# The output projection of a hybrid diffusion layer: the first 128 tokens' products ahead of the others, on four PSUM banks, one weight block read twice

## The chip, the cores and the metric

The kernel runs on one core of one Trainium2 chip. The metric is the device time of one execution in microseconds (us), from the first to the last instruction of the core. All numbers are fp32.

## The reference, cut to what matters

One layer over 256 latent tokens (two blocks of 128, t = 0 and 1, in the kernel) of width 2048. A mixing sub-layer (Fourier groups and a bidirectional state-space mixer, with 256 context tokens ahead of it) is projected by `w_out` and added; then an expert layer: each token picks 16 of 16384 experts in each of 8 heads, by top-16 over two sets of 128 keys, and needs the rows `u` and `v` of each expert picked.

```python
y_x = concatenate([fourier_branch(proj_x), y_x_ssm], -1) @ w_out      # (256, 2048) @ (2048, 2048)
x = x + gm_x * rms_norm(y_x, g_post_mix)
hx2 = modulate(rms_norm(x, g_pre_ffn), sf_x, cf_x)
# peer_ffn, for each block tb of 128 tokens:
q = (tb @ w_query).reshape(128, 8, 128)
s1, s2 = q[..., :64] . sub_keys_1, q[..., 64:] . sub_keys_2
idx, gate = top 16 of the sums of the top 16 of s1 and of s2, softmax
act = gelu(einsum('td,thkd->thk', tb, expert_u[idx]))
y_f = einsum('thk,thkd->td', gate * act, expert_v[idx])
x = x + gf_x * rms_norm(y_f, g_post_ffn)
```

The mean in `rms_norm(y_x)` runs over all 2048 columns of a token, so nothing behind the projection can start for a block of tokens before all four of its column blocks are there.

## The kernel before, in words

The program is written engine by engine, each engine's instructions in the order in which it executes them, with semaphores between them. Nothing is reordered: where an engine waits, all that is queued behind it waits too.

*The projection.* `w_out` is used in four column blocks n = 0..3 of 512 (4 MB each). A product (n, t) is 16 matmuls 128x128 by 128x512 into one PSUM bank, 8 over the Fourier half and 8 over the state-space half of the mixed channels. `OUT_ORDER` (L116) gives the order: (0,0), (0,1), (1,0), (2,0), (3,0), (1,1), and, behind the start of the query stage for t = 0, (2,1), (3,1). Product (n, t) goes to bank (n % 2) * 2 + t. ScalarE reads each finished product twice (`wo_out`, L858: squares with their sum at L862, copy at L863), but not before the last tile of `w_mod` has been used (`tail_used`, VectorE, L1155), since the two share memory. Two of the products have column sums of those `w_mod` tiles in their middle (`SUMS_AT`), which the vector of the second normalisation needs.

*The weights.* Wide blocks come through two ring slots of 4 MB (`RING`, L92; slot 0 or 1 by the index's parity), each in 4 loads of 1 MB issued by SyncE (`ring_load`, L370), as soon as the last product that used the slot's former block is done. Block 2 of `w_out` has places of its own (`apart`). The ring holds `w_out` blocks 0, 1, 3 (slots 1, 0, 1) and then the two halves of `w_query`: the first (heads 0 to 3) in slot 0, the second (heads 4 to 7) in slot 1. The first head's columns alone have a load of their own (`first_head`), for a query that comes early. SyncE's queue goes on with two stores of x1 behind the query blocks. A row of such a block is 512 numbers, 2 KB.

*Behind the projection.* `x1_make(t)` (VectorE, L1357) needs all four products of t; then ScalarE squares x1 (`x1_norm`, L871), VectorE makes h2 (`x1_variance`, `h2_make`), TensorE transposes h2 (L1960) and makes queries (L1977) and key scores (L1985). For t = 0 only head 0's query is made first, TensorE then does (2,1) and (3,1), and then the queries in the order `QUERIES`: heads 1, 2, 3 of t = 0, the transposes of h2 for t = 1, heads 0 to 3 of t = 1, heads 4 to 7 of both. ScalarE has `x1_norm(1)` in its program behind the evacuation of the second query (`query_out(1)`, L903).

*The stream.* VectorE routes unit 0 (head 0, t = 0; top-16 and indices), and from then on GpSimd gathers expert rows by indirect DMA (L594): one gather is 128 rows of 8 KB, 1 MB. Each u row is used by one dot product on VectorE (`dot`, L1449). The first 16 gathers go round four slots, so gather n waits for dot n - 4. `X1_AFTER`, `VARIANCE_AFTER`, `H2_AFTER`, `FIRST_KEYS_AFTER` and so on say behind which dot VectorE does the steps of t = 1 and the routing of unit 1. Gather 20 waits for 8 queries, gather 24 for all 16 (`gather_u`, L599), since their slots are the ring's. With gathers 20 to 23 go three half rows of v. After gather 24 the stream of u and v rows and of v tiles runs to the end of the kernel.

Of the kernel before, what the change touches and what calls it, by code (L numbers as in the profile page):

```python
# [26 lines left out]
P = 128  # L27
# [65 lines left out]
        + [("in", n * NQ) for n in range(4)]  # L93
        + [("out", n * NQ) for n in (0, 1, 3)]
        + [("query", n * NQ) for n in range(2)])
R_XBC, R_FZ, R_OUT, R_QUERY = 0, 3, 7, 10
RING_CHUNK = (0, 1, 3)
APART = 2
# [16 lines left out]
ROOT_G, ROOT_Y, ROOT_X, ROOT_F = 4, 6, 7, 10  # L115
OUT_ORDER = [(0, 0), (0, 1), (1, 0), (2, 0), (3, 0), (1, 1), (2, 1), (3, 1)]  # L116
OUT_AHEAD = 6
QUERIES = [0, 1, 2, 3, 8, 9, 10, 11, 4, 5, 6, 7, 12, 13, 14, 15]
# [3 lines left out]

ROWS_AT = (2, 0)
SUMS_AT = {(1, 0): 6, (2, 0): 7}
H2T_AT = 3
EXP_AT, SECOND_EXP_AT = 2, 8
X1_AFTER, VARIANCE_AFTER, H2_AFTER = 3, 4, 5
FIRST_KEYS_AFTER, FIRST_PAIRS_AFTER, FIRST_WEIGHTS_AFTER = 6, 8, 9
WEIGHTS_AFTER = 15
# [16 lines left out]
def build(nc, x, ctx_in, w_mod, w_in, w_fmix, w_out, w_query, k1t, k2t, expert_u, expert_v,  # L146
          cols_in, rows_in, cst_in, dft_in, iota_in, out):
    with ExitStack() as ctx:
# [54 lines left out]
        scores = [at(k, 2048).rearrange("p (u n) -> p u n", u=PH) for k in (96, 170)]  # L203
        uslot = [at(8 * s, D) for s in range(NU)]
        early = [at(k, D) for k in (112, 120, 128, 191, 104)]
# [161 lines left out]
        def _(sp):  # L367
            wide = {"in": w_in, "out": w_out, "query": w_query}

            def ring_load(j):  # L370

                i = j - 2
                if i >= R_OUT:
                    sp.wait_ge(wo_ps, OUT_ORDER.index((RING_CHUNK[i - R_OUT], 1)) + 1)
                elif i >= R_FZ:
                    sp.wait_ge(h_ps, 2 * (i - R_FZ + 1))
                elif i == R_XBC:
                    sp.wait_ge(beta_ps, 1)
                elif i > R_XBC:
                    sp.wait_ge(xbc_ps, 4 * (i - R_XBC + 1))  # L380
                elif j == R_XBC + 1:
                    sp.wait_ge(mod_ps, 4)
                name, c0 = RING[j]
                src = wide[name].rearrange("(k p) n -> p k n", p=P)[:, :, c0:c0 + NQ]
                for i in range(PIECES):
                    part = slice(i * KT // PIECES, (i + 1) * KT // PIECES)
                    sp.dma_start(wring[j % 2][:, part], src[:, part]).then_inc(ring_in[j % 2], 16)
# [81 lines left out]
            for t in range(2):  # L469
                sp.dma_start(xrow[t], x[t * P:(t + 1) * P, :]).then_inc(row_in[t], 16)  # L470
            for j in range(R_OUT + 2, R_QUERY):
                ring_load(j)
            sp.wait_ge(col_ps, 8)
# [6 lines left out]
            sp.dma_start(keys[64:P, :, NKEYS:2 * NKEYS], k2t).then_inc(keys_in, 16)  # L480
            for j in range(R_QUERY, len(RING)):
                ring_load(j)
# [191 lines left out]
        def _(act):  # L674
# [183 lines left out]
            def wo_out(n, t):  # L858
                act.wait_ge(wo_ps, OUT_ORDER.index((n, t)) + 1)
                ps = PS[:, (n % 2) * 2 + t, :]  # L860
                dst = yrow[t][:, n * NQ:(n + 1) * NQ]
                step(A(dst, ps, ACT.Square, accum_out=ysq[:, 4 * t + n:4 * t + n + 1]))  # L862
                A(dst, ps, ACT.Copy).then_inc(wo_evac, 1)  # L863
# [216 lines left out]
        def _(dve):  # L1080
# [277 lines left out]
            def x1_make(t):  # L1358
                dve.wait_ge(wo_evac, OUT_ORDER.index((3, t)) + 1)
                r = yss[:, t:t + 1]  # L1360
                step(V.tensor_reduce(r, ysq[:, 4 * t:4 * t + 4], AX.X, ALU.add))
                ts(r, r, 1.0 / D, EPS, ALU.mult, ALU.add).then_inc(var_ready, 1)
                dve.wait_ge(std_ready, ROOT_Y + 2 * t + 1)
                dve.wait_ge(grow_in, 32)
                step(V.reciprocal(r, r))
                step(stt(yrow[t], yrow[t], r, Grow[0], ALU.mult, ALU.mult))
                tt(xrow[t], xrow[t], yrow[t], ALU.add).then_inc(x1_ready, 1)
# [206 lines left out]
        def _(pe):  # L1574
# [332 lines left out]

            def out_weight(n, k):

                if n == APART:  # L1910
                    i = [k < k1 for _, k1 in APART_K].index(True)
                    return apart[i][:, k - APART_K[i][0], :]
                return wring[(R_OUT + RING_CHUNK.index(n)) % 2][:, k, :]

            def w_out(n, t, ks, start=True, stop=True):

                for k in ks:
                    cat = catF if k < 8 else catS
                    ins = M(PS[:, (n % 2) * 2 + t, :], cat[:, k % 8, t * P:(t + 1) * P], out_weight(n, k),  # L1919
                            start=(start and k == ks[0]), stop=(stop and k == ks[-1]))  # L1920
                return ins

            def out_product(n, t):

                if t == 0 and n == APART:
                    pe.wait_ge(late_in, 32 + 16 * len(APART_K))
                elif t == 0:
                    ring_wait(R_OUT + RING_CHUNK.index(n))
                if n >= 2:
                    pe.wait_ge(wo_evac, OUT_ORDER.index((n - 2, t)) + 1)  # L1930
                if (n, t) == (0, 0):
# [5 lines left out]
                    ins = w_out(0, 0, FOURIER, start=False)  # L1937
                elif (n, t) == (0, 1):
                    w_out(0, 1, FOURIER, stop=False)
                    pe.wait_ge(yt_evac, 2)  # L1940
                    ins = w_out(0, 1, SSM, start=False)
                else:
# [208 lines left out]
```

## Time and profile before

| | us |
|---|---|
| median of 3 runs | 1807.82 |
| lowest, highest | 1807.16, 1808.38 |
| profiled execution, its span | 1808.4 |

Busy time in the profiled execution:

| engine | us | share of the span |
|---|---|---|
| TensorE, matmuls | 1472.5 | 81% |
| VectorE | 1307.8 | 72% |
| GpSimd | 883.5 | 49% |
| ScalarE | 437.1 | 24% |

All DMA queues together moved 684.77 MB, 379 GB/s over the span. Of it 503 MB went through GpSimd's queue (q0), most of that expert rows; q1 is SyncE's. The share of an engine over the whole span says little here: the kernel has a mixing part of some 430 us, the projection and routing stage of some 190 us that the change touches, and the long stream behind it. Read the stage in order of time. In the timeline rows the columns are start, duration, engine, line, operation, and in brackets the idle time before it and what ended it. One fp32 matmul has two records, so a product of 16 matmuls is 32 records.

### The profile page before, as it was taken

What the parts mean: (1) busy time and instruction counts of PE and PEld (TensorE: products, weight loads), DVE (VectorE), ACT (ScalarE), POOL (GpSimd) and SP (SyncE); (2) the same over time, 40 slices, a digit from 0 to 9 for tenths busy, and PEclk for the clock granted to TensorE, in tenths of its full rate; (3) what the DMA queues carried; (4) which work ended last, traced back from release to release, by engine and by line L of the source; (5) the groups of instructions that cost most, each with busy time, mean ns of one, the idle gap of its engine ahead of it and who ended that gap; (6) DMA issues with size and microseconds to landing.
All of it is one profiled execution on the core that took longest, in us unless ns stands there. A gap on an engine that the chain in (4) does not pass through costs nothing.

```text
span 1808.4 us, 13738 instructions
## 1 busy us (share of the span) xinstructions
PE 1472.5 (81%) x4549; PEld 708.0 (39%) x4549; DVE 1307.8 (72%) x1687; ACT 437.1 (24%) x1176; POOL 883.5 (49%) x666
## 2 busy tenths in 40 slices
PE   6999999999998855656555665678999999989963
PEld 3344464556447711111111233345444444433320
DVE  3118888777249989999998989898556566656678
ACT  3011211120112412121122687787100000000010
POOL 0012242312013788887777888775545554522242
PEclk9999999999999976666668899889999999999985
DMA  9998997899649999999999999999999999999997
GB/s 362 387 387 291 334 369 261 324 343 363 230 150 390 386 397 419 418 419 419 419 419 417 417 391 400 408 356 383 415 413 412 412 413 414 417 418 417 417 421 314
DMA packets 166101, 684.77 MB, mean 379 GB/s; under 512 B 16464, under 2 KB 21136, under 8 KB 122768
## 3 DMA queue, kind: packets, MB, share of 16 engines
q0 software_dynamic: 92160, 503.36, 69.4%
q1 hardware_dynamic: 73440, 177.41, 25.9%
q10 hardware_dynamic: 432, 3.15, 0.4%
q8 instruction: 36, 0.59, 0.1%
q14 instruction: 33, 0.27, 0.0%
HBM read 679.56 MB, written 4.29 MB: 378 GB/s over the span
## 4 chain that ended last, share of the span: by engine, by line
DMA 36%; PE 26%; POOL 18%; DVE 10%; issue 5%; SPq 4%; ACT 1%; DVEq 0%; POOLq 0%; ACTq 0%
DMA arena<-in_expert_v,arena 27%; POOL arena L594 18%; PE PS L1754 6%; DMA arena<-in_expert_u,arena 6%; PE PS L1643 6%; PE PS L1919 4%; SPq L404 3%; DMA arena<-in_w_mod 3%; PE PS L1977 3%; DVE arena L1449 3%; DVE arena L1484 2%; PE PS L2005 2%; DVE arena L1494 1%; PE PS L1778 1%; SPq L392 1%
## 5 line engine op out<-in xcount | busy, mean ns | idle before, releaser
L1449 DVE CUSTOM_DVE_ANT_0 arena<-arena 128x2048 f32<-128x2048 f32 x256 | 578.9, 2288 | 96.7 <-DMA arena<-in_expert_u,arena 95.7
L594 POOL DMA_INDIRECT arena<-in_expert_v,arena x256 | 397.0, 1551 | 310.6 <-DVE arena L1494 116.1
L2005 PE MATMUL PS<-arena 128*128 128x512 f32 x512 | 344.6, 811 | 231.9 <-DMA arena<-in_expert_v,arena 225.9
L594 POOL DMA_INDIRECT arena<-in_expert_u,arena x256 | 390.3, 1525 | 213.0 <-issue 72.8
L2057 PE MATMUL PS<-arena 128*128 128x512 f32 x1024 | 455.2, 600 | 15.2 <-DMA arena<-in_expert_v 12.0
L2057 PEld LDWEIGHTS PS<-arena 128*128 128x128 f32 x1024 | 192.0, 191 | 277.8 <-issue 224.3
L2005 PEld LDWEIGHTS PS<-arena 128*128 128x128 f32 x512 | 112.6, 243 | 433.7 <-DMA arena<-in_expert_v,arena 334.5
L1155 DVE SCALAR_TENSOR_TENSOR arena<-arena 128x1024 f32<-128x1024 f32 x120 | 160.9, 1341 | 21.1 <-DMA arena<-in_w_mod 18.1
L524 POOL DMA_DIRECT2D arena<-in_w_mod x128 | 68.5, 537 | 211.8 <-DVE arena L1155 172.5
L1494 DVE SCALAR_TENSOR_TENSOR arena<-arena 128x2048 f32<-128x2048 f32 x51 | 119.9, 2351 | 69.3 <-DMA arena<-in_expert_v,arena 69.0
L1006 ACT ACTIVATE arena<-arena 128x4 f32<-128x4 f32 x64 | 12.9, 202 | 555.7 <-DVE arena L1449 488.8
L1484 DVE SCALAR_TENSOR_TENSOR arena<-arena 128x1024 f32<-128x1024 f32 x63 | 80.9, 1284 | 66.3 <-DMA arena<-in_expert_v,arena 65.1
L1919 PE MATMUL PS<-arena 128*128 128x512 f32 x256 | 112.7, 599 | 4.2 <-ACT arena L863 3.4
L1754 PE MATMUL PS<-arena 128*128 128x512 f32 x256 | 112.1, 596 | 0.0
L1643 PE MATMUL PS<-arena 128*128 128x512 f32 (+1 forms) x256 | 100.9, 553 | 0.0
L1919 PEld LDWEIGHTS PS<-arena 128*128 128x128 f32 x256 | 48.7, 192 | 64.2 <-issue 64.2
L1754 PEld LDWEIGHTS PS<-arena 128*128 128x128 f32 x256 | 48.9, 192 | 61.4 <-issue 61.4
L1643 PEld LDWEIGHTS PS<-arena 128*128 128x128 f32 x256 | 49.1, 195 | 47.3 <-issue 44.5
L1123 DVE TENSOR_TENSOR arena<-PS,arena 128x8 f32<-128x8 f32 x8 | 1.3, 166 | 85.8 <-PE PS L1609 85.8
L1977 PEld LDWEIGHTS PS<-arena 128*128 128x128 f32 x512 | 60.7, 196 | 1.1 <-issue 0.5
L1977 PE MATMUL PS<-arena 128*128 128x128 f32 x512 | 60.9, 278 | 0.0
L998 ACT ACTIVATE arena<-arena 128x128 f32<-128x128 f32 x128 | 45.0, 392 | 61.4 <-PE PS L2005 60.5
(261 smaller groups left out, 1343.7 us busy)
## 6 DMA issues: line engine op xcount, KB each, us to landing
arena<-in_w_mod POOLq DMA_DIRECT2D x128, 512.0 KB, 6.5
arena<-in_expert_v SPq DMA_DIRECT2D x128, 512.0 KB, 8.0
arena<-in_w_mod SPq DMA_DIRECT2D x32, 1024.0 KB, 14.4
arena<-in_w_in SPq DMA_DIRECT2D x28, 1024.0 KB, 14.4
arena<-in_w_out SPq DMA_DIRECT2D x15, 1024.0 KB, 14.1
arena<-in_w_query SPq DMA_DIRECT2D x9, 1024.0 KB, 12.6
arena<-in_x SPq DMA_DIRECT2D x4, 1024.0 KB, 10.3
arena<-cum_rows SPq DMA_DIRECT2D x4, 1024.0 KB, 9.6
```

Of the source, the lines that this page charges most:

```text
L524: nc.gpsimd.dma_start(slots[s], src).then_inc(tail_in[s], 16)
L594: nc.gpsimd.indirect_dma_start(slot, None, table, bass.IndirectOffsetOnAxis(ap=rows[:, n:n + 1], axis=0),).then_inc(arrived, 16)
L1155: ins = stt(acc, tile, s2[:, k, 0:1], acc, ALU.mult, ALU.add)
L1449: V.tensor_tensor_reduce(out=rows, in0=rows, in1=h2row[u // PH], scale=1.0, scalar=0.0, op0=ALU.mult, op1=ALU.add, accum_out=dots[:, u % B ...
L1484: ins = stt(a[:, 0:HALF], row, c, a[:, 0:HALF], ALU.mult, ALU.add)
L1494: ins = stt(a, row, c, a, ALU.mult, ALU.add)
L1643: ins = M(o, wring[j % 2][:, k, (b % 4) * P:(b % 4 + 1) * P], rhs, start=(k == 0), stop=(k == KT - 1))
L1754: ins = M(PS[:, j % 2, :], hT[:, 0, k, t * P:(t + 1) * P], wring[(R_FZ + c) % 2][:, k, :], start=(k == 0), stop=(k == KT - 1))
L1919: ins = M(PS[:, (n % 2) * 2 + t, :], cat[:, k % 8, t * P:(t + 1) * P], out_weight(n, k), start=(start and k == ks[0]), stop=(stop and k == ...
L1977: ins = M(PS[:, 4 + i % 2, 0:P], w, h2T[t][:, k, :], start=(k == 0), stop=(k == KT - 1))
L2005: ins = M(PS[:, b, :], diag_slot[m % DIAGS], slot[:, b * NQ:(b + 1) * NQ], start=(m == 0), stop=(m == BLK - 1))
L2057: ins = M(PS[:, 2 + 2 * blk + h, :], G[blk][:, i, :], tile[i % TILES][:, h * NQ:(h + 1) * NQ], start=(i == 0), stop=(i == NKEYS - 1 and bl ...
```

## The change

All of it lies in the order of the stage; no arithmetic changes.

- `OUT_ORDER` becomes (0,0), (1,0), (2,0), (3,0), (1,1), then, behind the first query, (2,1), (3,1), (0,1). Product i in that order uses bank i % 4, so the first four need no bank to be emptied.
- Slot 1 is free after (0,0) for block 3, slot 0 after (1,1). Block 0 is needed again for (0,1), so it is read a second time, into slot 0 (`RING` has one entry more). The two halves of `w_query` change slots: the first goes to slot 1 when (3,1) is done, the second to slot 0 when (0,1) is done. SyncE issues block 0's second load behind the key loads.
- The column sums move to (2,0) and (3,0), again the third and fourth product, and the transposition of the vector rows goes behind (3,0).
- On VectorE the steps of t = 1 go behind later dots: x1 behind dot 7 (3 before), its variance 8 (4), h2 9 (5), the keys of unit 1 9 (6), its pairs 11 (8), weights of unit 0 12 (9). ScalarE's second exponential goes behind query 6 (8).
- `uslot` lists the slots' places in the other order, since the other ring slot is free first.

```diff
@@ -91,10 +91,9 @@
 
 RING = ([("in", OFF_XBC + n * NQ) for n in range(3)]
         + [("in", n * NQ) for n in range(4)]
-        + [("out", n * NQ) for n in (0, 1, 3)]
+        + [("out", n * NQ) for n in (0, 1, 3, 0)]
         + [("query", n * NQ) for n in range(2)])
-R_XBC, R_FZ, R_OUT, R_QUERY = 0, 3, 7, 10
-RING_CHUNK = (0, 1, 3)
+R_XBC, R_FZ, R_OUT, R_QUERY = 0, 3, 7, 11
 APART = 2
 APART_K = [(0, 4), (4, 8), (8, 12), (12, 15), (15, 16)]
 
@@ -113,19 +112,22 @@
 LATE_QUOTA = [4, 1, 1, 4, 1, 21]
 LATE = 5
 ROOT_G, ROOT_Y, ROOT_X, ROOT_F = 4, 6, 7, 10
-OUT_ORDER = [(0, 0), (0, 1), (1, 0), (2, 0), (3, 0), (1, 1), (2, 1), (3, 1)]
-OUT_AHEAD = 6
+OUT_ORDER = [(0, 0), (1, 0), (2, 0), (3, 0), (1, 1), (2, 1), (3, 1), (0, 1)]
+OUT_AHEAD = 5
+OUT_RING = {(0, 0): R_OUT, (1, 0): R_OUT + 1, (1, 1): R_OUT + 1, (3, 0): R_OUT + 2, (3, 1): R_OUT + 2, (0, 1): R_OUT + 3}
+OUT_FREES = {R_OUT: (0, 0), R_OUT + 1: (1, 1), R_OUT + 2: (3, 1), R_OUT + 3: (0, 1)}
+OUT_DONE = [4, 8]
 QUERIES = [0, 1, 2, 3, 8, 9, 10, 11, 4, 5, 6, 7, 12, 13, 14, 15]
 TAIL_QUOTA = [0, 1, 3, 5, 8, 8, 8, 7, 7, 7, 6, 4]
 
 
 
-ROWS_AT = (2, 0)
-SUMS_AT = {(1, 0): 6, (2, 0): 7}
+ROWS_AT = (3, 0)
+SUMS_AT = {(2, 0): 6, (3, 0): 7}
 H2T_AT = 3
-EXP_AT, SECOND_EXP_AT = 2, 8
-X1_AFTER, VARIANCE_AFTER, H2_AFTER = 3, 4, 5
-FIRST_KEYS_AFTER, FIRST_PAIRS_AFTER, FIRST_WEIGHTS_AFTER = 6, 8, 9
+EXP_AT, SECOND_EXP_AT = 2, 6
+X1_AFTER, VARIANCE_AFTER, H2_AFTER = 7, 8, 9
+FIRST_KEYS_AFTER, FIRST_PAIRS_AFTER, FIRST_WEIGHTS_AFTER = 9, 11, 12
 WEIGHTS_AFTER = 15
 
 
@@ -201,7 +203,7 @@
         keys = at(152, 2048).rearrange("p (h n) -> p h n", h=PH)
         qT = at(162, 2048).rearrange("p (h t) -> p h t", h=PH)
         scores = [at(k, 2048).rearrange("p (u n) -> p u n", u=PH) for k in (96, 170)]
-        uslot = [at(8 * s, D) for s in range(NU)]
+        uslot = [at(k, D) for k in (32, 40, 48, 56, 0, 8, 16, 24)]
         early = [at(k, D) for k in (112, 120, 128, 191, 104)]
         vslot = [at(64 + 4 * s, HALF) for s in range(V_SLOTS)]
         bring = [at(k, D) for k in (152, 199, 170, 64, 72, 0, 8, 16, 24)]
@@ -371,7 +373,7 @@
 
                 i = j - 2
                 if i >= R_OUT:
-                    sp.wait_ge(wo_ps, OUT_ORDER.index((RING_CHUNK[i - R_OUT], 1)) + 1)
+                    sp.wait_ge(wo_ps, OUT_ORDER.index(OUT_FREES[i]) + 1)
                 elif i >= R_FZ:
                     sp.wait_ge(h_ps, 2 * (i - R_FZ + 1))
                 elif i == R_XBC:
@@ -468,8 +470,7 @@
             sp.wait_ge(yg_ready, 2)
             for t in range(2):
                 sp.dma_start(xrow[t], x[t * P:(t + 1) * P, :]).then_inc(row_in[t], 16)
-            for j in range(R_OUT + 2, R_QUERY):
-                ring_load(j)
+            ring_load(R_OUT + 2)
             sp.wait_ge(col_ps, 8)
             sp.dma_start(first_head, w_query.rearrange("(k p) n -> p k n", p=P)[:, :, 0:P]).then_inc(keys_in, 16)
             rows_store(2, 2 * KT, 4 * KT)
@@ -478,7 +479,7 @@
             sp.wait_ge(keys_zero, 1)
             sp.dma_start(keys[0:64, :, 0:NKEYS], k1t).then_inc(keys_in, 16)
             sp.dma_start(keys[64:P, :, NKEYS:2 * NKEYS], k2t).then_inc(keys_in, 16)
-            for j in range(R_QUERY, len(RING)):
+            for j in range(R_OUT + 3, len(RING)):
                 ring_load(j)
 
             for t in range(2):
@@ -857,7 +858,7 @@
 
             def wo_out(n, t):
                 act.wait_ge(wo_ps, OUT_ORDER.index((n, t)) + 1)
-                ps = PS[:, (n % 2) * 2 + t, :]
+                ps = PS[:, OUT_ORDER.index((n, t)) % 4, :]
                 dst = yrow[t][:, n * NQ:(n + 1) * NQ]
                 step(A(dst, ps, ACT.Square, accum_out=ysq[:, 4 * t + n:4 * t + n + 1]))
                 A(dst, ps, ACT.Copy).then_inc(wo_evac, 1)
@@ -1356,7 +1357,7 @@
             for t in range(2):
                 dve.wait_ge(row_in[t], 32)
             def x1_make(t):
-                dve.wait_ge(wo_evac, OUT_ORDER.index((3, t)) + 1)
+                dve.wait_ge(wo_evac, OUT_DONE[t])
                 r = yss[:, t:t + 1]
                 step(V.tensor_reduce(r, ysq[:, 4 * t:4 * t + 4], AX.X, ALU.add))
                 ts(r, r, 1.0 / D, EPS, ALU.mult, ALU.add).then_inc(var_ready, 1)
@@ -1905,29 +1906,31 @@
 
             FOURIER, SSM = list(range(8)), list(range(8, KT))
 
-            def out_weight(n, k):
+            def out_weight(n, t, k):
 
                 if n == APART:
                     i = [k < k1 for _, k1 in APART_K].index(True)
                     return apart[i][:, k - APART_K[i][0], :]
-                return wring[(R_OUT + RING_CHUNK.index(n)) % 2][:, k, :]
+                return wring[OUT_RING[n, t] % 2][:, k, :]
 
             def w_out(n, t, ks, start=True, stop=True):
 
                 for k in ks:
                     cat = catF if k < 8 else catS
-                    ins = M(PS[:, (n % 2) * 2 + t, :], cat[:, k % 8, t * P:(t + 1) * P], out_weight(n, k),
+                    ins = M(PS[:, OUT_ORDER.index((n, t)) % 4, :], cat[:, k % 8, t * P:(t + 1) * P], out_weight(n, t, k),
                             start=(start and k == ks[0]), stop=(stop and k == ks[-1]))
                 return ins
 
             def out_product(n, t):
 
-                if t == 0 and n == APART:
+                if n == APART:
                     pe.wait_ge(late_in, 32 + 16 * len(APART_K))
-                elif t == 0:
-                    ring_wait(R_OUT + RING_CHUNK.index(n))
-                if n >= 2:
-                    pe.wait_ge(wo_evac, OUT_ORDER.index((n - 2, t)) + 1)
+                else:
+                    ring_wait(OUT_RING[n, t])
+                if OUT_ORDER.index((n, t)) >= 4:
+                    pe.wait_ge(wo_evac, OUT_ORDER.index((n, t)) - 3)
+                if n == 2 and t == 0:
+                    pe.wait_ge(yt_evac, 2)
                 if (n, t) == (0, 0):
                     pe.wait_ge(pq_evac, GROUPS)
                     pe.wait_ge(yt_evac, 1)
@@ -1935,10 +1938,6 @@
                     y_transposes(1)
                     pe.wait_ge(yf_evac, GROUPS)
                     ins = w_out(0, 0, FOURIER, start=False)
-                elif (n, t) == (0, 1):
-                    w_out(0, 1, FOURIER, stop=False)
-                    pe.wait_ge(yt_evac, 2)
-                    ins = w_out(0, 1, SSM, start=False)
                 else:
                     ins = w_out(n, t, FOURIER, stop=False)
                     if (n, t) in SUMS_AT:
```

## Rows read from the trace of the kernel before

**Rows 1.** The page: the span.

```profile
span 1808.4 us, 13738 instructions
```

**Rows 2.** Stretches: span, length, engines' busy us, PEclk, DMA share, GB/s.

```profile
500.00:515.00 15.00, 15.00 (x36) 6.40 (x34) 9.35 (x9) 3.69 (x7) 0.00 (x0) 1.00 0.00 0
...
598.00:618.80 20.80, 20.80 (x178) 20.37 (x176) 20.06 (x35) 3.48 (x11) 14.72 (x9) 1.00 1.01 415
...
630.00:650.00 20.00, 11.48 (x21) 4.04 (x21) 14.50 (x24) 5.57 (x14) 16.95 (x11) 0.84 0.96 369
...
1300.00:1780.00 480.00, 448.50 (x992) 186.47 (x991) 298.38 (x209) 18.77 (x73) 211.49 (x158) 0.97 1.02 416
```

**Rows 3.** Timeline of TensorE, 422 to 479 us.

```profile
422.90 7.11 PE L1919 MATMUL PS<-arena 128*128 128x512 f32 x16 [0.81 <-DVE arena L1342]
...
430.72 27.63 PE L1919 MATMUL PS<-arena 128*128 128x512 f32 x64
...
470.39 8.50 PE L1919 MATMUL PS<-arena 128*128 128x512 f32 x16 [3.39 <-ACT arena L863]
```

**Rows 4.** Timeline of TensorE, 522 to 620 us.

```profile
522.23 27.63 PE L1919 MATMUL PS<-arena 128*128 128x512 f32 x64
549.70 7.31 PE L1977 MATMUL PS<-arena 128*128 128x128 f32 x64
...
566.07 3.68 PE L1960 MATMUL PS<-arena 128*128 128x128 f32 x16 [4.62 <-DVE arena L1380]
569.54 5.00 PE L1977 MATMUL PS<-arena 128*128 128x128 f32 x32
...
618.43 1.23 PE L1985 MATMUL PS<-arena 128*128 128x256 f32 x4
```

**Rows 5.** Timeline of VectorE: last w_mod tile; h2 of t = 0, 1.

```profile
467.56 1.28 DVE L1155 SCALAR_TENSOR_TENSOR arena<-arena 128x1024 f32<-128x1024 f32 x1 [0.77 <-DMA arena<-in_w_mod]
...
511.06 2.35 DVE L1378 SCALAR_TENSOR_TENSOR arena<-arena 128x2048 f32<-128x2048 f32 x1
...
563.72 2.29 DVE L1380 TENSOR_TENSOR arena<-arena 128x2048 f32<-128x2048 f32 x1
```

**Rows 6.** Timeline of ScalarE: (3,0), query 1, square of x1.

```profile
501.43 0.60 ACT L862 ACTIVATE arena<-PS 128x512 f32<-128x512 f32 x1 [12.36 <-PE PS L1919]
...
553.47 0.28 ACT L903 ACTIVATE arena<-PS 128x128 f32<-128x128 f32 x1 [1.64 <-PE PS L1977]
556.77 1.91 ACT L871 ACTIVATE arena<-arena 128x2048 f32<-128x2048 f32 x1 [3.03 <-DVE arena L1367]
```

**Rows 7.** Timeline of GpSimd: gather 0 and gather 24.

```profile
533.41 1.00 POOL L594 DMA_INDIRECT arena<-in_expert_u,arena  x1 [62.69 <-DVE arena L1426]
...
618.87 0.93 POOL L594 DMA_INDIRECT arena<-in_expert_u,arena  x1 [3.71 <-PE PS L1977]
```

**Rows 8.** DMA queues, 456 to 466 us: packets, MB, share.

```profile
q0 software_dynamic: 683, 2.52, 63.9%
q1 hardware_dynamic: 739, 1.48, 39.2%
```

**Rows 9.** DMA issue, 517 to 518 us: KB, us to landing.

```profile
arena<-in_w_query SPq DMA_DIRECT2D x1, 1024.0 KB, 13.1
```

**Rows 10.** DMA queues, 556 to 560 us.

```profile
q0 software_dynamic: 169, 1.23, 75.5%
q1 hardware_dynamic: 172, 0.34, 22.7%
```

**Rows 11.** DMA queues, 562 to 566 us.

```profile
q1 hardware_dynamic: 719, 1.42, 93.6%
```

**Rows 12.** DMA queues, 552 to 554 us.

```profile
q1 hardware_dynamic: 272, 0.56, 78.7%
```

**Rows 13.** DMA issue, 553 to 558 us: KB, us to landing.

```profile
arena<-in_w_query SPq DMA_DIRECT2D x1, 1024.0 KB, 26.4
```

**Rows 14.** Timeline of SyncE's issues from 553 us.

```profile
551.41 7.88 SPq L387 DMA_DIRECT2D arena<-in_w_query  x1
```

## The prediction

> **What bounds the kernel now.** I read the page first: the span is 1808.4 us [rows 1]. Then the stretches: from about 598 us to the end the DMA engines are never free, at 415 to 416 GB/s [rows 2], because the expert rows and tiles that are still to come are more bytes than the queues can move. So from there on a microsecond is won or lost only by when that stream starts. Between 500 and 515 us the DMA engines do nothing at all [rows 2]; that hole is where this stage could give something back. Then I read TensorE, ScalarE, VectorE and GpSimd in order of time through the hole. One product of the output projection takes 13.8 us (two in 27.63) [rows 3, 4]. The fourth product of before waited 3.39 us for a bank [rows 3], since ScalarE may not empty banks before the last w_mod tile is used (468.8) [rows 5]. The last product needed by the first 128 tokens, (3,0), ends as ScalarE reads it, at 501.43 [rows 6]; the first gather is issued at 533.41 [rows 7]. The last thing in the stage that the stream waits for is the end of the sixteenth query: gather 24 waits 3.71 us and is issued at 618.87, right behind TensorE's 618.4 [rows 4, 7]. I call that end Q16. Before it only 24 gathers and three half rows can be issued, whatever else is early; all the rest of the stream comes after it. So the change is worth what it does to Q16.
>
> **The front of the stage.** From the start of (0,0) at 422.90 to 501.43 lie 78.5 us: five products (69.1), the wait (3.4), 1.6 that the clock's fall after it cost (8.50 for a half product instead of 6.9 [rows 3]), and transposes and column sums. The change takes (0,1), the wait and the slow half out: 13.8 + 3.4 + 1.6 = 18.8 us. No product now waits for a bank until (1,1), at about 482, when ScalarE has long begun.
>
> Against it: the load of block 3 is now issued at (0,0)'s end (437.7), not (0,1)'s (451.5). It runs beside the w_mod tiles the whole way, at 1.48 MB in 10 us against their 2.52 [rows 8]: 4.19 MB by 0.148 is 28.3 us, so from 439.7 to 468, where TensorE wants it at 466.9. I take 2 us with landing (ends: 0, as VectorE leaves the queue dips, and 5). The tiles, which now share for longer, end near 471 instead of 468.8; the column sums that need them come at 475: nothing. The row vector for h2 is now stored only after (3,0) but has the 9.6 us from 501.43 to 511.06 [rows 5, 6] before its use: nothing, or 1. So (3,0) and all that follows for the first tokens come 16.8 us earlier: first gather 516.6, end of (3,1) 533.1 (549.9 before), end of (0,1) 546.9.
>
> **The second read of block 0.** SyncE issues it after (1,1), at 498.4, into the empty DMA queues [rows 2]; such a block landed 13.1 us after its last piece's issue there [rows 9], so by 512 to 514, before the first gather, and TensorE wants it at 533. Cost 0. If that cover were gone it would be 4.19 MB at 415 GB/s, 10.1 us.
>
> **The first query block, the term that decides.** Before, it went to slot 0, free after (1,1): it was issued into idle queues [rows 9], two products and a chain of h2 ahead of its use. Now slot 0 gets block 0 again, and the query block goes to slot 1, which block 3 holds until the end of (3,1), the last product but one. Now it is issued at 533.1 with 13.8 us of product over it, and with gathers in flight. Behind it on SyncE's queue stand the second query block and the two stores of x1. What a 2 KB row gets beside 8 KB gather rows is in the trace: from 556 to 560 us the gather queue moved 169 packets and SyncE's 172, that is 1.23 MB against 0.34 [rows 10]. One for one in packets is 3.6 to 1 in bytes: 43 weight packets a us. Alone they go at 719 in 4 us, 180 a us [rows 11]. The block has 2048.
>
> The Trainium skill, page "DMA: Bandwidth & Descriptors", section "Queues, rings and completion order", says that each DMA engine goes round the queues that have work, a packet at a time. It speaks against this change, since it gives the queue with the smaller packets less of the bytes; one for one with rows of 8 and 2 KB would be 0.082 MB a us, the row gives 0.085, the sum is the same within 1 us. The trace agrees [rows 10].
>
> How long are there gathers beside it? Before, dots 0 to 3 were followed by x1 and h2 of the second tokens, and the gather queue ran dry. Now dots 4 to 7 follow at once, and each frees one of four slots. Gathers 6 to 11 (1.05 MB each) then keep the queue full: 6.3 MB at 0.31 MB a us is 20.4 us. So: bytes start some 2 us after issue, and before gather 6 flows the weights get 272 packets in 2 us [rows 12], to 537.1; 20.4 us at 43 is 877, to 557.5; 899 are left. By then VectorE has made x1 of the second tokens and stands at its variance: that waits for ScalarE's square, which is queued behind the evacuation of query 1, and so behind this very block. Only gather 12 is still coming: 3.4 us with 146 packets, then 753 at 180, 4.2 us. Landing L = 557.5 + 7.6 = 565.1. Bounds: the block that before was issued at 549.9 had its last piece issued at 551.41 and landed 26.4 us later [rows 13, 14], 27.9 in all, beside fewer gathers but also 1 MB of stores (2.5 us); so not below 533.1 + 25.4 = 558.5. Above, 568, if later loads of the same queue get ahead on some engines. I take 565.
>
> **From L to Q16.** TensorE has nothing from 546.9 to L. Query 1's start to its evacuation took 3.8 us (549.70 to 553.47) [rows 4, 6]; from the square at 556.77 to h2's end at 566.0 9.3 us, one dot included [rows 5, 6]. So h2 of the second tokens is ready at L + 13.1. It had been 16.1 after the last product's end. After the idle stretch the clock is low, as before at 566.07 after 4.62 us idle, where a query took 5.00 instead of 3.7 [rows 4]: 1.3. From the transposes to Q16 it was 52.4 us (566.07 to 618.43) [rows 4], 3.0 of it slow clock, which this time falls before and not in it: 49.4. Q16 = L + 63.8, or 66.8 if it falls in both: 628.9 against 618.4, that is 10.5 later.
>
> **What of it comes back.** From 630 to 650 us before moved 369 GB/s, not 415 [rows 2]: 2.2 us lost, in part since VectorE still had old dots to do. With all 24 dots done at Q16 I take 1 back (0 to 2.2). The stream after it is full at both ends of the kernel and holds the same bytes, so the rest goes through to the end. Sum: +9.5 us on 1808.4, 1817.9; the median of the runs shown is 0.6 below the profiled execution, so 1817.3.
>
> **The rivals.**
> - *The block lands under its cover.* If it lands by 548 or so, (0,1) hides all but nothing of it, Q16 is the second tokens' h2 (546.9 + 16.1) and 52.4: 615.4, 3.0 earlier, 5.0 if block 3 is not late either. With 1 us back that is 1802 to 1804. It decides from L = 555.6 down (there Q16 is 1 us later than before and the end the same). For it: the idle-queue landing of 13.1 us [rows 9], less than the 13.8 of cover. Against it: the packets one for one [rows 10], the landing beside gathers [rows 13], and that gathers are in flight from 516.6 on. Chance 0.12. The Trainium skill, same page, section "Bandwidth", has 1 MB in 6.15 us and 16 MB in 79, about 20 us for 4 MB as an estimate, nearer to this rival than the 27.9 us beside gathers; its table is of a load with the queues to itself, as that of the 13.1 us was.
> - *The queue runs dry early.* If gathers are freed more slowly than I took (VectorE late, slow issues of GpSimd), the weights get 180 packets a us sooner and land at 554 to 558: Q16 within 3 us of before, 1807 to 1811. Chance 0.13.
> - *Q16 does not decide.* The earlier first gathers then shift the stream itself by up to the idle DMA time they fill, some 10 us: 1798. Against: gather 24's wait [rows 7]. Chance 0.04. That the change does not do what it says is part of this one; the order is written out by hand, so I give it nothing of its own.
> - *Late at the front as well.* Block 3 costs 5 us, or the second read of block 0 slips beside the gathers: 1823 to 1828. Chance 0.06.
>
> **How the numbers follow.** Forecast, block late and Q16 later by 5 to 15 us: 0.65; its own range is 1812 to 1823. The range 1804.5 to 1823.5 leaves out the first rival's better part (0.09), the third (0.04) and the fourth (0.05). By cases, with 0.03 of the first rival and 0.04 of the forecast counted as no change: a measurement of this kernel tells about 0.2% (3.6 us) from no change; faster 0.13, same 0.20, slower 0.67.
>
> **What would show it.** Front: no bank wait, (3,0) evacuated at 482 to 487, first gather at 514 to 519. Term that decides: the first query block issued near 533, its last piece landing some 30 us later, TensorE idle from 547 to about 565 with a low clock behind it, packets of both queues one for one meanwhile. End: Q16 near 629, gather 24 right behind it, with GpSimd waiting some 10 us and DMA idle before it; from there the same rate as before. It is wrong if TensorE starts query 1 within 2 us of (0,1)'s end, or if gather 24 does not wait for Q16.

## The result, and the profile after

| | before | after |
|---|---|---|
| median, us | 1807.49 (4 runs, 1804.77 to 1808.38) | 1824.99 (4 runs, 1823.42 to 1831.12) |
| ratio to before | | 1.0112 (95%: 1.0088 to 1.0136) |
| profiled execution, span | 1808.4 | 1829.1 |

The changed kernel is 1.1% slower: 17.5 us by the medians, some 20 us by the ratio. 1817.3 was forecast, with 1823.5 as the upper end. The profiled execution of after is the longest of its four runs, so 20.7 us between the two profiles is more than the runs as a whole show.

The timeline of TensorE after the change, from the start of (0,0) to the start of the stream (columns as before; in this kernel L1920 is the projection, L1959 the transposes of h2, L1976 the queries, L1984 the key scores):

```profile
423.02 7.11 PE L1920 MATMUL PS<-arena 128*128 128x512 f32 x16 [0.81 <-DVE arena L1343]
...
473.18 8.88 PE L1920 MATMUL PS<-arena 128*128 128x512 f32 x16 [6.06 <-DMA arena<-in_w_out]
...
511.55 41.36 PE L1920 MATMUL PS<-arena 128*128 128x512 f32 x96
571.67 9.32 PE L1976 MATMUL PS<-arena 128*128 128x128 f32 x64 [18.76 <-DMA arena<-in_w_query]
...
586.86 1.97 PE L1959 MATMUL PS<-arena 128*128 128x128 f32 x16 [1.43 <-DVE arena L1381]
...
636.29 1.23 PE L1984 MATMUL PS<-arena 128*128 128x256 f32 x4
```

Set against [rows 3, 4]: the wait for a bank (3.39 us) ahead of the fourth product is gone, and in its place the fourth product, now (3,0), waits 6.06 us for block 3's load. The three products behind the first query run without a break to 552.9, and then TensorE stands 18.76 us for the first query block. The wait for h2 (4.62 us before) is 1.43. Q16, the end of the sixteenth query, is at 636.3 instead of 618.4.

TensorE's losses between the start of (0,0) and Q16 add up to this. Before, it lost 3.39 us to the bank and 1.39 to the slow half product behind that wait, 4.62 to h2 and 2.98 to slow matmuls behind it: 12.4 us. After, it loses 6.06 and 1.77 at block 3, 18.76 and 2.01 at the query block, and 1.43 at h2: 30.0 us. The difference, 17.6 us, is all but 0.1 of the 17.7 by which the stage is longer from the start of (0,0) to Q16.

The other engines show the same from their side: ScalarE's read of (3,0) and the square of x1 of the second tokens (against [rows 6]), and GpSimd's gathers 0 and 24 (against [rows 7]).

```profile
490.74 0.60 ACT L863 ACTIVATE arena<-PS 128x512 f32<-128x512 f32 x1 [12.58 <-PE PS L1920]
...
577.46 0.28 ACT L904 ACTIVATE arena<-PS 128x128 f32<-128x128 f32 x1 [22.58 <-PE PS L1976]
577.63 1.90 ACT L872 ACTIVATE arena<-arena 128x2048 f32<-128x2048 f32 x1
```

```profile
522.74 1.00 POOL L595 DMA_INDIRECT arena<-in_expert_u,arena  x1 [46.53 <-DVE arena L1427]
...
636.73 2.43 POOL L595 DMA_INDIRECT arena<-in_expert_u,arena  x1 [11.87 <-PE PS L1976]
```

(3,0) is read 10.7 us earlier than before and gather 0 goes out 10.7 us earlier. But the square of x1, in ScalarE's program behind the evacuation of query 1, comes only at 577.63, and gather 24 has waited 11.87 us for TensorE when it goes, 17.9 us later than before. The chain of work that ended last (start, us, what) puts the loss into one line of the stage:

```profile
511.71 27.48 PE PS L1920 x64
539.21 0.37 SPq L389
...
541.06 30.57 DMA arena<-in_w_query
571.67 5.76 PE PS L1976 x32
```

(3,1) ends at 539.2, SyncE issues the four loads within 2 us, and the last one lands 30.57 us after its issue. Before, no load stood in the chain here. It went from (3,1)'s end through ScalarE and VectorE (x1, its square, h2 of the second tokens) to the transposes, and query 1, which TensorE began at 549.70 without a pause [rows 4], was not on it:

```profile
549.90 0.70 ACT arena L862 x2
...
563.72 2.30 DVE arena L1380
566.07 3.68 PE PS L1960 x16
```

The rest of the kernel did not change by more than it does from one execution to the next: from Q16 to the end it is 1190.0 us before and 1192.8 after, and that stretch was between 1184 and 1193 in all profiles of this study.

### The profile page after: what moved, and what is told of

Same layout as the page of the kernel before. It is cut to its first block, busy times and chain, and to the rows that moved or that the text cites. A ratio compares the mean times of both kernels' runs of the same rounds, so it can differ in the third digit from the quotient of the medians.

```text
span 1829.1 us, 13745 instructions
## 1 busy us (share of the span) xinstructions
PE 1475.3 (81%) x4549; PEld 706.7 (39%) x4549; DVE 1307.6 (71%) x1687; ACT 437.0 (24%) x1176; POOL 899.8 (49%) x666
## 4 chain that ended last, share of the span: by engine, by line
DMA 37%; PE 26%; POOL 19%; DVE 7%; issue 5%; SPq 5%; ACT 1%; DVEq 0%; POOLq 0%; ACTq 0%
DMA arena<-in_expert_v,arena 28%; POOL arena L595 19%; PE PS L1755 6%; PE PS L1644 5%; DMA arena<-in_expert_u,arena 4%; SPq L406 3%; PE PS L1920 3%; PE PS L1976 3%; PE PS L2004 2%; DVE arena L1485 2%; DMA arena<-in_w_out 2%; DMA arena<-in_w_query 2%; DMA arena<-in_w_mod 2%; DVE arena L1450 1%; DVE arena L1495 1%
## 5 line engine op out<-in xcount | busy, mean ns | idle before, releaser
L595 POOL DMA_INDIRECT arena<-in_expert_u,arena x256 | 402.1, 1571 | 220.3 <-DVE arena L1450 75.7
L1920 PE MATMUL PS<-arena 128*128 128x512 f32 x256 | 113.0, 601 | 6.9 <-DMA arena<-in_w_out 6.1
L1976 PE MATMUL PS<-arena 128*128 128x128 f32 x512 | 61.6, 280 | 18.8 <-DMA arena<-in_w_query 18.8
L1920 PEld LDWEIGHTS PS<-arena 128*128 128x128 f32 x256 | 48.8, 193 | 67.2 <-issue 60.2
L1976 PEld LDWEIGHTS PS<-arena 128*128 128x128 f32 x512 | 61.2, 197 | 20.2 <-DMA arena<-in_w_query 19.6
```

The lines of the kernel that those rows point to most:

```text
L595: nc.gpsimd.indirect_dma_start(slot, None, table, bass.IndirectOffsetOnAxis(ap=rows[:, n:n + 1], axis=0),).then_inc(arrived, 16)
L1920: ins = M(PS[:, OUT_ORDER.index((n, t)) % 4, :], cat[:, k % 8, t * P:(t + 1) * P], out_weight(n, t, k), start=(start and k == ks[0]), stop ...
L1976: ins = M(PS[:, 4 + i % 2, 0:P], w, h2T[t][:, k, :], start=(k == 0), stop=(k == KT - 1))
```

## The experiments

The start of (0,0) lay between 417.5 and 428.8 us in the profiles, whatever the kernel, so the stage is measured from there. The first table line is the kernel before; "wait" is TensorE's for the first query block.

| kernel | block 3 wait | gather 0 | wait | Q16 | gather 24 | ratio to before (95%) |
|---|---|---|---|---|---|---|
| before | none (bank 3.39) | 110.5 | none | 195.5 | 196.0 | 1 |
| after | 6.06 | 99.7 | 18.76 | 213.3 | 213.7 | 1.0112 (1.0088 to 1.0136) |
| e1_dots_before | 4.49 | 98.6 | 5.89 | 199.1 | 201.5 | 1.0036 (1.0020 to 1.0052) |
| e2_quarter_query | 4.69 | 99.0 | 3.12 | 196.5 | 196.9 | 0.9989 (0.9970 to 1.0008) |
| e3_quarter_block0 | 4.61 | 98.8 | 19.43 | 213.0 | 213.4 | 1.0092 (1.0066 to 1.0118) |
| e4_quarter_block3 | none | 91.6 | 17.69 | 203.6 | 204.1 | 1.0057 (1.0035 to 1.0079) |
| e5_banks_alone | none | 105.5 | none | 189.2 | 189.7 | 0.9958 (0.9942 to 0.9974) |
| e6_banks_h2 | none | 105.5 | none | 185.7 | 189.7 | 0.9964 (0.9944 to 0.9983) |
| e7_swap | 4.44 | 98.9 | none | 197.0 | 197.4 | 1.0021 (1.0004 to 1.0038) |
| e8_block3_late | 6.38 | 101.2 | 17.79 | 214.8 | 215.3 | 1.0107 (1.0074 to 1.0139) |
| e9_rows_1kb | 4.88 | 98.9 | 20.07 | 213.4 | 213.8 | 1.0115 (1.0084 to 1.0147) |

All but the waits and ratios are us from the start of (0,0) in the profiled execution of each. 0.001 of the ratio is 1.8 us. A profiled execution can lie up to 10 us off its kernel's median (e5 1807.4 beside 1797.8, e4 1809.1 beside 1816.4, e7 1800.9 beside 1808.2), so the columns tell of the stage and the ratio of the kernel.

Up to (3,0) six of these kernels, after, e1, e2, e3, e7 and e9, are the same. Block 3's wait is 4.44 to 4.88 us in five of them; the 6.06 of after's profile stands alone.

### Dots as before: fewer gathers beside the query block

```diff
-X1_AFTER, VARIANCE_AFTER, H2_AFTER = 7, 8, 9
-FIRST_KEYS_AFTER, FIRST_PAIRS_AFTER, FIRST_WEIGHTS_AFTER = 9, 11, 12
+X1_AFTER, VARIANCE_AFTER, H2_AFTER = 3, 4, 5
+FIRST_KEYS_AFTER, FIRST_PAIRS_AFTER, FIRST_WEIGHTS_AFTER = 6, 8, 9
```

> The changed kernel with VectorE's steps of the second tokens back behind dots 3, 4 and 5 (keys 6, pairs 8, weights 9), as before the change; all else as changed. My theory (the first query block lands late because gathers run beside it, packet for packet, and Q16, the end of the sixteenth query, follows it): VectorE now stops for x1 behind dot 3, so only gathers 4 to 7 are in flight beside the block and the gather queue runs dry near 549 us; the block then moves alone and lands near 557 instead of 571.5, Q16 comes near 622 instead of 636.3, the kernel takes about 14 us less than the changed one, 1809 to 1813. Rival (the block's landing is set by its issue behind (3,1) and by SyncE's queue, not by gathers): landing stays within 2 us of 571, the time within 3 us of 1825. Rival (Q16 does not set the end; the dots do): landing earlier, time the same or longer, since the dots are later.

Measured: 1812.97 us, ratio 1.0036, beside 1.0112. TensorE of this kernel, at the first query block and at Q16:

```profile
553.85 9.15 PE L1976 MATMUL PS<-arena 128*128 128x128 f32 x64 [5.89 <-DMA arena<-in_w_query]
...
618.29 1.23 PE L1984 MATMUL PS<-arena 128*128 128x256 f32 x4
```

From the start of (0,0) (419.21 here) query 1 begins at 134.6 us, in after at 148.6; Q16 comes 14.2 us earlier, as expected. Not one load was moved: only VectorE stops behind dot 3, so gathers 8 to 12 are not issued while the block is on its way. These are 5.2 MB, 13 us at the queue's rate, and the landing came 14.0 us earlier. Both rivals fall. Gather 24 did not follow Q16 all the way: it goes 2.4 us behind it, without a wait for TensorE, right behind the gathers ahead of it:

```profile
618.51 1.91 POOL L595 DMA_INDIRECT arena<-in_expert_v,arena  x1 [0.30 <-issue]
620.72 1.91 POOL L595 DMA_INDIRECT arena<-in_expert_u,arena  x1 [0.30 <-issue]
```

The run also shows that most of the loss (14.2 of 17.7 us at Q16) hangs on the constants that put four more dots ahead of x1: more dots mean more gathers beside the weights.

### A quarter of each load in turn

Each of these three kernels leaves out three quarters of one load and makes the products or queries of that block in part from other numbers; all waits stay. The edit is the same for the three, with `j ==` `R_QUERY`, `R_OUT + 3` (block 0, second time) and `R_OUT + 2` (block 3):

```diff
+                    if j == R_QUERY:
+                        part = slice(part.start, part.start + 1)
                     sp.dma_start(wring[j % 2][:, part], src[:, part]).then_inc(ring_in[j % 2], 16)
```

> The changed kernel with each of the four loads of the first query block cut to one of its four rows of 128 channels, so that 1 MB comes instead of 4 MB; the rest of the slot keeps what block 3 left there, so these queries are made from other numbers. Everything waits and runs as in the changed kernel. My theory: the block (512 packets) lands before (0,1) ends at 553, TensorE goes on without a stop, Q16 is set by h2 of the second tokens: 553 + 16 + 52, near 621 instead of 636.3, and the kernel takes 1808 to 1812. Rival (the loss is in the 4 MB more that are read, or in the later dots): 1822 or more, since only 3 MB are gone, 7.5 us at the stream's rate if the queues were the bound there: 1817.

Measured: 1805.53 us, ratio 0.9989. This is below the expected 1808 to 1812, although TensorE, which was to go on without a stop, still waited 3.12 us for the 1 MB that is left. Q16 came 16.8 us earlier than in after, 1.0 later than before, and the kernel is no longer to be told from before. The price of the first query block's late landing is thus as large as nearly the whole loss of the change, 16.8 of 17.7 us. (With block 3's cost, below, the parts are more than the loss, since the change also takes out waits of before.) The rival of the bytes (1817) falls.

> The changed kernel with the second load of block 0 cut to a quarter in the same way (1 MB instead of 4 MB; product (0,1) is made in part from other numbers). My theory: this load runs in an idle stretch (505 to 520 us) and is long there when (0,1) wants it, so nothing changes: within 3 us of the changed kernel's 1825. Rival (the second read is paid for at the stream's rate): 3.1 MB at 0.415 MB a us is 7.5 us less, 1817.

Measured: 1823.97 us, ratio 1.0092 beside 1.0112, the intervals overlap, and Q16 is 0.3 us from after's. The second read of 4 MB costs nothing that shows.

> The changed kernel with the load of block 3 cut to a quarter in the same way (product (3,t) is made in part from other numbers). It measures the step that I had put at 2 us: TensorE waited 6.06 us for this block and its clock fell behind it. My theory: the wait and the slow half product go, 8 us, (3,1) ends near 531 instead of 539.2, and as the query block's landing follows (3,1) by the same 32 us, Q16 comes 8 us earlier and the kernel takes 1816 to 1819. Rival (time gained at the front is eaten by a longer landing beside the gathers, or by the w_mod tiles): under 4 us gained, 1821 or more.

Measured: 1816.42 us, ratio 1.0057. The wait of 6.06 us and the slow half product are gone, gather 0 and Q16 come 8.1 and 9.7 us earlier than in after, and the wait for the query block is about the same, 17.69. So what block 3 costs at the front goes through to the end in full, and the time from (3,1) to the landing (31.4 us here, 32.5 in after) does not depend on the front.

### Block 3 issued as late as before

```diff
+            sp.wait_ge(wo_ps, 2)
             ring_load(R_OUT + 2)
```

> The changed kernel with SyncE's load of block 3 held back behind (1,0), to about 451.5 us as before the change, instead of behind (0,0), 437.9. My new theory of the front: until 470 us the DMA queues are full, and this block and the last w_mod tiles are 12 MB that end together at about 470 whatever the order, so issuing the block 13.6 us earlier had gained nothing; the last piece lands within 3 us of the changed kernel's 473, TensorE waits 6 to 9 us for it, and the kernel takes 1824 to 1829. Rival (the block moves at its share of 0.148 MB a us from its issue on, as I had reckoned): it lands 10 us or more later than in the changed kernel and the kernel takes 1833 or more. The w_mod tiles should end earlier, near 469.

Measured: 1824.13 us, ratio 1.0107. SyncE's issues and TensorE's wait:

```profile
450.77 7.81 SPq L389 DMA_DIRECT2D arena<-in_w_out  x4
```

```profile
472.64 10.04 PE L1921 MATMUL PS<-arena 128*128 128x512 f32 x16 [6.38 <-DMA arena<-in_w_out]
```

The loads are issued at 450.8 instead of 437.9 and the wait is 6.38 us, against 6.06 in after and 4.44 to 4.88 in the other five kernels with after's front. So 13 us of later issue cost 2 us at most, and the rival's 10 fall. What moved is the other traffic: VectorE's last w_mod tile begins 44.4 us from the start of (0,0) instead of 50.0. The queues of before and after from 440 to 470 us say why (packets, MB, share):

```profile
q0 software_dynamic: 2122, 7.71, 69.1%
q1 hardware_dynamic: 1672, 3.35, 30.4%
```

```profile
q0 software_dynamic: 2110, 7.66, 65.0%
q1 hardware_dynamic: 2102, 4.25, 37.3%
```

The first fence is before, the second after. Block 3 and the last w_mod tiles are some 12 MB, which at 397 GB/s take 30 us from 440 on, in whatever order they go. The late issue leaves the queues less full for a while, 369 GB/s in this stretch before and 370 in e8, which fits the 2 us. In before no engine waited for the block, since (3,0) was a product later: its last load, issued at 453.3, landed 20.3 us later, at 473.6.

### Packets half as large

```diff
+                    if j == R_QUERY:
+                        for half in range(2):
+                            col = slice(half * NQ // 2, (half + 1) * NQ // 2)
+                            sp.dma_start(wring[j % 2][:, part, col], src[:, part, col]).then_inc(ring_in[j % 2], 16)
+                        continue
```

(and TensorE's wait counts the 64 more)

> The changed kernel with each 1 MB load of the first query block issued as two of 0.5 MB, of 256 columns each, so that its packets are 1 KB instead of 2 KB. My theory (gathers and weights go packet for packet): while both queues are full the block gets as many packets as the gathers, so half the bytes of before, near 0.045 MB a us instead of 0.09; some 0.9 MB more are left when the gathers stop, and alone 1 KB packets move no faster in bytes: the block lands 3 to 7 us later, Q16 with it, 1827 to 1833. Rival (shares go by bytes, or the block is paced by SyncE's queue or by its last engine): landing within 1.5 us of the changed kernel's, time within 2 us of it.

Measured: 1824.98 us, ratio 1.0115: nothing, where 3 to 7 us were expected. The share did what it should. Queues from 546 to 560 us, first after, then this kernel:

```profile
q0 software_dynamic: 621, 4.56, 78.9%
q1 hardware_dynamic: 630, 1.25, 23.6%
```

```profile
q0 software_dynamic: 683, 4.97, 85.4%
q1 hardware_dynamic: 778, 0.77, 16.0%
```

In after it is one for one, 621 to 630. With packets of 1 KB SyncE's queue got a few more packets than the gathers but far fewer bytes, 0.77 MB against 4.97. Yet from the first issue of the block to query 1's start it was 33.8 us, in after 32.5. The gathers got the bytes that the block lost and were done sooner, and then the block was alone for longer. From 560 to 565 us, first after, then this kernel:

```profile
q0 software_dynamic: 169, 1.12, 54.6%
q1 hardware_dynamic: 447, 0.89, 47.0%
```

```profile
q1 hardware_dynamic: 1746, 1.73, 108.9%
q0 software_dynamic: 5, 0.01, 0.4%
```

So the count of packets says who waits while both are there; when the slower one is done is set by the bytes of both together, as long as the other's are bounded. The numbers are the rival's (landing within 1.5 us, time within 2), but of its reasons the first, shares by bytes, is refuted by the packets above, and the second, that SyncE's queue sets the pace, by e1; that one slow DMA engine sets the end is not excluded. My rule for the landing was too narrow, and its number came right since the sum of bytes was right: in after the queues moved 11.84 MB from 541 to 570 us, nearly all of it gathers and this block, at 408 GB/s.

```profile
DMA packets 3163, 11.84 MB, mean 408 GB/s; under 512 B 180, under 2 KB 180, under 8 KB 2230
...
q0 software_dynamic: 1055, 7.64, 63.8%
q1 hardware_dynamic: 2108, 4.20, 38.5%
```

### The other order of the last products

```diff
-OUT_ORDER = [(0, 0), (1, 0), (2, 0), (3, 0), (1, 1), (2, 1), (3, 1), (0, 1)]
+OUT_ORDER = [(0, 0), (1, 0), (2, 0), (3, 0), (1, 1), (3, 1), (2, 1), (0, 1)]
```

(and the six constants of the first experiment)

> The changed kernel with (3,1) ahead of (2,1), so that slot 1 is free and the first query block is issued 13.8 us earlier, and with VectorE's steps behind dots 3, 4, 5 and 6, 8, 9 as before. Gather 1 waits for (2,1), so the gathers but one start 13.8 us later and the block has the queues nearly to itself. My theory: block issued at 525, landed by 541; (0,1) ends at 553 with the block there, TensorE does not stop; Q16 near 553 + 16 + 52 = 621 to 623; time 1809 to 1814. If landing beside gathers is not what costs, the stop of about 18 us stays and the time is 1820 or more.

Measured: 1808.23 us, ratio 1.0021. The block, issued at 519.2 with one gather beside it, no longer stops TensorE, and Q16 is at 197.0 from the start of (0,0), 1.5 later than before; the time is just under the expected 1809 to 1814. Here the first gathers come no earlier than before (gather 1 waits for (2,1)), so of the change little more is left than block 3's wait in place of the bank's: 4.44 us and 2.57 of slow half product, against 3.39 and 1.39.

### The banks alone

```diff
-                if n >= 2:
-                    pe.wait_ge(wo_evac, OUT_ORDER.index((n - 2, t)) + 1)
+                if OUT_ORDER.index((n, t)) >= 4:
+                    pe.wait_ge(wo_evac, OUT_ORDER.index((n, t)) - 3)
```

(in the kernel before, and `OUT_ORDER.index((n, t)) % 4` for the bank in both places)

> The kernel before with one part of the change alone: product i in the order goes to bank i % 4 and waits for ScalarE only from the fifth on. Order of the products, loads and dots as before. Theory (Q16 sets the start of the stream, and the front of the stage sets Q16): the wait of 3.39 us at the fourth product and 1.6 us of slow clock behind it go, everything up to Q16 comes 5 us earlier, and so does the end: 1802.5, ratio 0.9972. Rival (the time is taken up again by the next wait, of the transposes for h2 of the second tokens, or by the second query block): within 1 us of before.

Measured: 1797.78 us beside 1805.52, ratio 0.9958. TensorE of this kernel:

```profile
436.65 27.63 PE L1919 MATMUL PS<-arena 128*128 128x512 f32 x64
465.82 13.98 PE L1919 MATMUL PS<-arena 128*128 128x512 f32 x32
481.34 7.11 PE L1919 MATMUL PS<-arena 128*128 128x512 f32 x16
...
566.98 3.63 PE L1960 MATMUL PS<-arena 128*128 128x128 f32 x16 [4.63 <-DVE arena L1380]
```

No wait for a bank, no slow half product; the wait for h2 stays at 4.63 us. Q16 is 6.3 us earlier than before and the kernel 7.6 by the ratio, where 5 were expected. The bank wait and its slow half product are 4.8 of the 6.3, and 1.3 come from less slow clock behind the same wait for h2. This one part of the change is worth having, and it is faster than both kernels.

> As e5_banks_alone, and h2 of the second tokens behind dot 4 with its variance (dot 5 behind it, not in between). Theory: dot 5 (2.2 us) leaves the chain of x1, square, variance, h2 that TensorE waits for with 4.6 us idle at 566 us; about 1.9 us of it is gained, so Q16 and the end come 7 us earlier than before: 1800.6, ratio 0.9961. Rival: ScalarE's square is as long as the dot and nothing is gained over e5.

The edit is `H2_AFTER = 4`. Measured: 1800.44 us, ratio 0.9964, not to be told from the banks alone (0.9958). The wait for h2 fell from 4.63 to 2.77 us and Q16 came another 3.5 us earlier, but gather 24 did not follow it:

```profile
608.00 1.23 PE L1985 MATMUL PS<-arena 128*128 128x256 f32 x4
```

```profile
607.56 1.92 POOL L594 DMA_INDIRECT arena<-in_expert_u,arena  x1 [0.30 <-issue]
609.78 1.90 POOL L594 DMA_INDIRECT arena<-in_expert_v,arena  x1 [0.30 <-issue]
```

The first row is gather 23, the second the last of the three half rows; gather 24 follows at 611.99 without a wait for TensorE. That is 189.7 us from the start of (0,0), and in e5 it was 189.7 too, there right behind Q16, after 2.65 us of waiting for it. So 6 us ahead of before Q16 stops being what the stream waits for, and the gathers ahead of gather 24, one behind the other, take over. In e5 GpSimd was ready for gather 24 some 2.4 us sooner than in e6; whether the later dot 5 is the reason was not tried, so at most 2.4 us are left to gain over e5 by Q16 alone.

## Why the prediction was right or wrong

**Direction and mechanism: right.** Slower was the likeliest (0.67), and by the step that was called the one that decides. What the time follows is the start of gather 24: against before, it and the time by the ratio agree to within 3 us in all ten kernels (gather 24 first: after 17.7 and 20.2; e1 5.5 and 6.5; e4 8.1 and 10.3; e5 -6.3 and -7.6; e6 -6.3 and -6.5; e7 1.4 and 3.8). In nine of the eleven kernels gather 24 waited for Q16. In e1 and e6 it did not: there GpSimd's own gathers were last, 2.4 and 4.0 us behind Q16. "Q16 decides" had been put without that limit.

**The landing of the first query block: right in size.** From (3,1)'s end to query 1 it was 31.9 us by the prediction (533.1 to 565) and 32.5 in the trace (539.2 to 571.67). That the gathers beside it would be those up to number 12 was right, and so was ScalarE's square stuck behind query 1. The reason given was half right: packets do go about one for one, but e9 shows that the landing follows the bytes of both queues, not the share. So the share was not what made the number right, and with other packet sizes the same working would have missed.

**The front: the term that was mis-sized.** This is the step that failed: "I take 2 us with landing (ends: 0 and 5)" for block 3. The wait was 6.06 us (4.44 to 4.88 in the five other kernels with this front), and the half product behind it took 8.88 us instead of 7.11 (9.26 to 9.68 in the five), the same slow clock that I had just credited as gained with the bank wait. Wait and slow clock together cost 7.8 us instead of 2. So the first tokens' products came 10.7 us earlier, not 16.8, and (3,1) ended at 539.2 instead of 533.1: 6.1 of the 7.4 us by which Q16 was off (636.3 against 628.9). I had divided the block's bytes by its share from a window and started the clock near its issue, which gave 468; it landed at 473.1. What the rows of before held was the total: everything queued from 440 us on was 12 MB, gone at 470 at the earliest. The last 3 us are not in that sum either: from 470 to 473 both queues together moved only 52 packets, and what held these up is not shown. e8 shows that 13 us of issue time were worth 2 us at most.

**From L to Q16**: 63.8 forecast, 64.6 measured (571.67 to 636.3), with one slow stretch, not two, as taken.

**What comes back**: 1 us was taken, none came. In the first 13.7 us behind Q16 the queues of after moved 280 GB/s, and those of before 380; after's started empty, behind GpSimd's long wait. First after, then before:

```profile
636.30:650.00 13.70, 8.06 (x17) 3.47 (x16) 6.66 (x6) 12.69 (x45) 8.99 (x6) 0.75 0.74 280
```

```profile
618.40:632.10 13.70, 8.05 (x16) 3.48 (x16) 13.32 (x25) 12.65 (x45) 9.61 (x7) 0.75 0.99 380
```

These 100 GB/s over 13.7 us are 1.4 MB, some 3 us at the stream's 415 GB/s, so the start costs where 1 us was to come back.

That VectorE had no old dots left to do brought nothing that could be seen; what else holds the stream in its first 14 us was not tried.

**The second read of block 0**: nothing, as reckoned (e3). **The last w_mod tile**: 471 forecast, 474.3 measured (473.06 and 1.28), still without cost, as the column sums came at 481.9.

**The range.** The measured 1825 is above 1823.5. "Late at the front as well", 1823 to 1828, had been given 0.06 and left out; it is the case that came. Its 5 us for block 3 were made around the same share, and the clock behind the wait was left out of them; with it the front cost 6.7 to 7.8 us in the six kernels that have it.

## What to carry to other kernels

When a load is moved into a stretch in which the DMA queues are full, reckon with the bytes of all that is queued until it must be there, not with its own size, its share or its time of issue; an earlier issue gains little there (here 2 us at most of 13), and work that frees buffers for other loads (here four more dots) pushes it back. When an order is changed so that one chain starts earlier, look at what takes over the last free slot: the chain of the second half was the one that the rest waited for, and it lost its prefetch. And try the parts alone: the four banks, without the new order, are 0.4% faster than before.

## What the runs showed of the hardware

Two queues that are both full shared the DMA engines nearly packet for packet over three different pairs of row sizes: 4 and 2 KB (1047 to 1105 packets from 450 to 465 us in after), 8 and 2 KB (621 to 630, and before 169 to 172 [rows 10]), 8 and 1 KB (683 to 778, the least even). The Trainium skill, page "DMA: Bandwidth & Descriptors", section "Queues, rings and completion order", has the turns of each DMA engine go by packets, and the three pairs agree. That the landing hardly moved between 2 and 1 KB (32.5 and 33.8 us) is no contradiction to it, but I had not drawn it from it.

After a wait of 18.76 us TensorE's next two queries took 9.32 us instead of 7.31, and its granted clock was 0.50 (1.2 GHz) from 571.67 to 575. After the 6.06 us the half product took 8.88 instead of 7.11, after 3.39 us before 8.50 [rows 3], and in e8 after 6.38 us 10.04 and after 17.79 us 10.35 for the two queries. The slow clock cost 1.4 to 3.0 us each time, and hardly more after the waits that were three times as long:

```profile
571.67:575.00 3.33, 3.33 (x15) 3.33 (x16) 0.00 (x0) 0.00 (x0) 0.00 (x0) 0.50 1.06 388
```
